# Norm stage of a decoder layer: transfers in another order, last row sums taken singly, first row in column thirds

## The reference, cut to what matters

```python
mod = jax.nn.silu(c) @ p['w_ada'] + p['b_ada']
sh_m, sc_m, g_m, sh_f, sc_f, g_f = [m[:, None, :] for m in jnp.split(mod, 6, axis=-1)]
xn = rmsnorm(x, p['rms_mix_g']) * (1.0 + sc_m) + sh_m
mix, k_rows, v_rows, s_new = token_mixer(xn, pos, p, attend, recur)
```

## Time and profile before

| | us |
|---|---|
| median of 3 runs | 2231.82 (2231.39 to 2233.82) |
| profiled execution, own time | 2233.89 |
| profiled execution, span from first to last instruction | 2232.1 |
| TensorE busy in the span | 2204.0 |
| mean granted TensorE clock | 0.999 of full speed |

### The profile page before, as it was taken

How to read it: one execution, slowest core, us unless ns; L and a number is a source line. 1 busy time by engine, 2 the same in 40 slices (tenths; PEclk the granted TensorE clock), 3 DMA queues, 4 the chain that set the end, 5 groups by cost and what they waited for, 6 DMA issues and landing times. The chain is left out here.

```text
span 2232.1 us, 48427 instructions
## 1 busy us (share of the span) xinstructions
PE 2204.0 (99%) x19103; PEld 2118.4 (95%) x19103; DVE 1517.7 (68%) x2529; ACT 1204.8 (54%) x2499; POOL 988.5 (44%) x1186
## 2 busy tenths in 40 slices
PE   7999999999999999999999999999999999999999
PEld 6899999999999999999898999999999999999999
DVE  5767677776767676775767425318988888876534
ACT  6667676767767676766443421125566666644110
POOL 1147272745555472727322124441256565635431
PEclk9999999999999999999999999999999999999999
DMA  8222222122222222222789523112354555485212
GB/s 311 67 65 81 67 88 67 59 87 76 80 71 85 74 72 68 88 67 97 299 307 363 212 51 124 38 57 94 122 185 174 188 185 191 172 313 193 86 48 96
DMA packets 103515, 288.37 MB, mean 129 GB/s; under 512 B 18426, under 2 KB 26490, under 8 KB 103290
## 3 DMA queue, kind: packets, MB, share of 16 engines
q1 hardware_dynamic: 102138, 281.09, 35.6%
q10 hardware_dynamic: 1152, 4.19, 0.5%
HBM read 213.18 MB, written 63.77 MB: 124 GB/s over the span
## 5 line engine op out<-in xcount | busy, mean ns | idle before, releaser
L173 PE MATMUL ps<-xn_hi,h_w_hi 128*128 128x344 f32 x1680 | 550.1, 327 | 2.3 <-PEq L206 0.9
L173 PE MATMUL ps<-xn_lo,h_w_hi 128*128 128x344 f32 x1680 | 536.6, 319 | 0.0
L173 PE MATMUL ps<-xn_hi,h_w_lo 128*128 128x344 f32 x1680 | 536.5, 319 | 0.0
L173 PEld LDWEIGHTS ps<-xn_hi,h_w_hi 128*128 128x128 f32 x1680 | 317.1, 189 | 20.7 <-issue 12.8
L173 PEld LDWEIGHTS ps<-xn_lo,h_w_hi 128*128 128x128 f32 x1680 | 315.8, 188 | 0.6
L173 PEld LDWEIGHTS ps<-xn_hi,h_w_lo 128*128 128x128 f32 x1680 | 315.8, 188 | 0.0
L1314 POOL TENSOR_TENSOR h_w_lo<-h_w_raw,h_w_hi 128x1024 fp32r<-128x1024 f32 x58 | 139.9, 2413 | 356.7 <-DVE h_a_E L1528 192.2
L3279 DVE SCALAR_TENSOR_TENSOR x<-ps,keep_mod,x 128x344 f32<-128x344 f32 x168 | 94.1, 570 | 162.6 <-PE ps L3116 99.7
L3116 PE MATMUL ps<-f_act_lo,f_d_hi 128*128 128x344 f32 x528 | 169.4, 321 | 0.0
L3116 PE MATMUL ps<-f_act_hi,f_d_lo 128*128 128x344 f32 x528 | 168.8, 320 | 0.0
L3116 PE MATMUL ps<-f_act_hi,f_d_hi 128*128 128x344 f32 x528 | 168.4, 319 | 0.2 <-DVE x L3279 0.2
(11 more groups left out here) (494 smaller groups left out, 6706.9 us busy)
## 6 DMA issues: line engine op xcount, KB each, us to landing
h_w_raw<-in_w_in SPq DMA_DIRECT2D x72, 512.0 KB, 3.5
y_rows<-f_y SPq DMA_DIRECT2D x44, 516.0 KB, 2.6
f_y_pair<-y_rows SPq DMA_DIRECT2D x22, 1032.0 KB, 5.3
h_d_ada_w<-in_w_ada SPq DMA_DIRECT2D x32, 512.0 KB, 3.8
g_vp<-in_cache_v SPq DMA_DIRECT2D x32, 512.0 KB, 6.0
f_a<-in_w_ffn SPq DMA_DIRECT2D x57, 256.0 KB, 2.6
g_kp<-in_cache_k SPq DMA_DIRECT2D x28, 512.0 KB, 7.8
h_w_raw<-in_w_mix SPq DMA_DIRECT2D x24, 512.0 KB, 3.5
```

Of the source, the lines that this page charges most:

```text
L173: ins = eng.matmul(out, w[:, k * P:(k + 1) * P], x[:, k, columns], start=(k == 0 and n == 0), stop=(k == n_k - 1 and n == 2))
```

## The change

- Transfers: x's rows 2 to 7 in one go; then the vectors, ada(0), the first two weights and ada(1) to ada(7), and all else behind them.
- Sums: pairs 0 to 2 as before; rows 6 and 7 are summed by TensorE each for itself.
- ScalarE rounds weight 0 (`split(0)`) between read_ada(0) and add_bias(0), no longer between the squares; VectorE rounds weight 1; weight 2 is rounded behind row 3. The two exponentials of the small vectors move behind row 4, VectorE's part of them (`exponents`, `bounds`) to rows 3 and 6.
- Row 0 is multiplied, rounded, reduced to its remainder and multiplied by the weights by column thirds, and stands in TensorE's list ahead of ada(2) and ada(3). VectorE copies ada(1) out of PSUM.
- ScalarE now does add_bias(k + 1) and read_ada(k + 2) behind row k.

```diff
-            load_x(2)
-            load_x(3)
-            load_w(0)
-            for k in range(4, KT):
+            for k in range(2, KT):
                 load_x(k)
             sp.dma_start(c["vec"][:, :], a["vec"]).then_inc(vec_in.sem, 16)
+            load_ada(0)
+            load_w(0)
             load_w(1)
-            load_ada(0)
-            for k in range(1, 5):
+            for k in range(1, KT):
                 load_ada(k)
...
-            split(0)
             for k in range(4, KT):
                 square(k)
-            act.wait_ge(lam_s.sem, 1)
-            act.activation(c["lam"][:, 0:2], c["lam"][:, 4:6], ACT.Exp).then_inc(lam_e.sem, 1)
-            act.wait_ge(lb_s.sem, 1)
-            act.activation(lw[:, 3:5, :], lw[:, 1:3, :], ACT.Exp).then_inc(lb_e.sem, 1)
-            split(1)
...
             read_ada(0)
-            read_ada(1)
+            split(0)
             add_bias(0)
-            read_ada(2)
-            add_bias(1)
             for k in range(KT):
...
+                if k == 0:
+                    for j in range(NP):
+                        act.activation(hi[:, 0, cols(j)], x[:, 0, cols(j)], ACT.Copy).then_inc(high.sem, 1)
+                else:
+                    act.activation(hi[:, k, :], x[:, k, :], ACT.Copy).then_inc(high.sem, 1)
                 if k == 1:
+                    read_ada(2)
+                if k + 1 < KT:
+                    add_bias(k + 1)
+                if 0 < k and k + 2 < KT:
+                    read_ada(k + 2)
+                if k == 3:
                     split(2)
...
+            def row_sums(k):
+                pe.wait_ge(squared.sem, k + 1)
+                for j in range(NP):
+                    ins = pe.matmul(SP_[:, j, 0:TH], mean[:, :], sq[k % 4][:, cols(j)], start=False, stop=(k == KT - 1))
+                    if k == KT - 1:
                         ins.then_inc(summed.sem, 1)
...
+            def first_pieces():
+
+                for t in range(2):
+                    pe.wait_ge(w_hi.sem, t + 1)
+                    pe.wait_ge(w_lo.sem, t + 1)
+                    for j in range(NP):
+                        pe.wait_ge(high.sem, j + 1)
+                        pe.wait_ge(low.sem, j + 1)
+                        row_products(0, t, j)
+                    if t == 0:
+                        pick(1)
...
-            for p in range(KT // 2):
+            for p in range(KT // 2 - 1):
                 sums(p)
+            row_sums(KT - 2)
+            row_sums(KT - 1)
             pe.wait_ge(csil.sem, 1)
             ada(0)
-            keep_clock(2)
-            ada(1)
+            keep_clock(3)
             pe.wait_ge(pick_ready.sem, 1)
             pick(0)
+            keep_clock(8)
+            ada(1)
             keep_clock(2)
+            pe.wait_ge(lnd.sem, NP)
+            first_pieces()
             ada(2)
-            keep_clock(1)
-            pick(1)
-            keep_clock(3)
-            pe.wait_ge(lnd.sem, NP)
-            for k in range(KT):
+            pick(2)
+            ada(3)
+            for k in range(1, KT):
                 if k + 3 < KT:
                     ada(k + 3)
...
             def rows(k):
 
-                ch(dve.tensor_tensor(x[:, k, :], x[:, k, :], rs[:, :], ALU.mult))
+                if k == 0:
+                    for j in range(NP):
+                        dve.wait_ge(rstd.sem, j + 1)
+                        ch(dve.tensor_tensor(x[:, 0, cols(j)], x[:, 0, cols(j)], rs[:, cols(j)], ALU.mult))
+                else:
+                    ch(dve.tensor_tensor(x[:, k, :], x[:, k, :], rs[:, :], ALU.mult))
+                if k == 1:
+                    dve.wait_ge(ada_done.sem, 2)
+                    copy(dve, av[1][:, :], X[:, 1, 0:2 * P]).then_inc(ada_read.sem, 1)
+                    rest(0)
...
             rows(0)
+            dve.wait_ge(w_in[1].sem, 16)
+            dve.wait_ge(w_hi.sem, 1)
+            copy(dve, early["hi"][1][:, :], early["raw"][1][:, :]).then_inc(w_hi.sem, 1)
             for k in range(1, KT):
                 rows(k)
-                rest(k - 1)
+                if k > 1:
+                    rest(k - 1)
+                if k == 3:
+                    exponents()
+                if k == 6:
+                    bounds()
```

More of the change, by code:

```diff
@@ L265, in _ @@
                 sp.dma_start(c[n][:, :], a[n]).then_inc(kept.sem, 16)
-            load_ada(5)
             for n in ("blk", "cos"):
@@ L337, in _ @@
                 act.wait_ge(scaled.sem, k + 1)
-                act.activation(hi[:, k, :], x[:, k, :], ACT.Copy).then_inc(high.sem, 1)
-                if k == 1:
-                    split(2)
[L341 to L344, removed]
+                if k == 0:
[3 more added lines that the diff above has]
+                    act.activation(hi[:, k, :], x[:, k, :], ACT.Copy).then_inc(high.sem, 1)
+                if k == 1:
+                    read_ada(2)
[4 more added lines that the diff above has]
+                if k == 3:
+                    split(2)
+                if k == 4:
+                    act.wait_ge(lam_s.sem, 1)
+                    act.activation(c["lam"][:, 0:2], c["lam"][:, 4:6], ACT.Exp).then_inc(lam_e.sem, 1)
+                    act.wait_ge(lb_s.sem, 1)
+                    act.activation(lw[:, 3:5, :], lw[:, 1:3, :], ACT.Exp).then_inc(lb_e.sem, 1)
         @block.tensor
@@ L350, in sums @@
                 for j in range(NP):
-                    ins = pe.matmul(SP_[:, j, 0:TH], mean[:, :], sq[2 * p % 4][:, cols(j)], start=(p == 0), stop=(p == KT // 2 - 1))
-                    if p == KT // 2 - 1:
+                    ins = pe.matmul(SP_[:, j, 0:TH], mean[:, :], sq[2 * p % 4][:, cols(j)], start=(p == 0), stop=False)
+                ins.then_inc(ms_used.sem, 1)
+            def row_sums(k):
[3 more added lines that the diff above has]
+                    if k == KT - 1:
                         ins.then_inc(summed.sem, 1)
-                if p < KT // 2 - 1:
-                    ins.then_inc(ms_used.sem, 1)
             def ada(k):
@@ L379, in keep_clock, with row_products @@
                     pe.matmul(G[:, 0, 0:P], mean[:, :], mean[:, :], start=True, stop=True)
-            def pieces(k):
[L383 to L391, removed]
+            def row_products(k, t, j):
+                n, w = EARLY_PIECES.index((t, j)), slice(k * P, (k + 1) * P)
+                for q, (wp, xp) in enumerate(((early["hi"], hi), (early["hi"], lo), (early["lo"], hi))):
+                    pe.matmul(first[n], wp[t][:, w], xp[:, k, cols(j)], start=(k == 0 and q == 0), stop=(k == KT - 1 and q == 2))
@@ new lines, in first_pieces @@
+            def first_pieces():
[8 more added lines that the diff above has]
+                        pick(1)
+            def pieces(k):
+                pe.wait_ge(high.sem, k + NP)
+                pe.wait_ge(low.sem, k + NP)
+                for t, j in EARLY_PIECES:
+                    row_products(k, t, j)
@@ L403, in _ @@
+            first_pieces()
             ada(2)
-            keep_clock(1)
-            pick(1)
-            keep_clock(3)
-            pe.wait_ge(lnd.sem, NP)
-            for k in range(KT):
+            pick(2)
+            ada(3)
+            for k in range(1, KT):
                 if k + 3 < KT:
                     ada(k + 3)
-                if k == 0:
-                    keep_clock(1)
                 if k + 2 < KT:
                     pick(k + 2)
-                if k == 0:
-                    keep_clock(6)
@@ L448, in _ @@
             dve.wait_ge(vec_in.sem, 16)
[L449 to L473, removed]
-            def rows(k):
-                ch(dve.tensor_tensor(x[:, k, :], x[:, k, :], rs[:, :], ALU.mult))
+            def exponents():
+                lv = vec[:, VEC["lam"][0]:VEC["lam"][0] + 4 * DH].rearrange("p (c s n) -> p c s n", c=2, s=2)
+                ch(dve.tensor_tensor(tmp[:, :, :], lv[:, :, 0, :], lv[:, :, 1, :], ALU.mult))
+                ch.sync()
+                dve.tensor_reduce(c["lam"][:, 4:6], tmp[:, :, :], AX.X, ALU.add).then_inc(lam_s.sem, 1)
+                lb0 = VEC["lb"][0]
+                l0, l1 = vec[:, lb0:lb0 + H], vec[:, lb0 + H:lb0 + 2 * H]
+                ch(dve.tensor_tensor(lw[:, 0, :], l0, l1, ALU.max))
+                ch.sync()
+                ch(dve.tensor_tensor(lw[:, 1, :], l0, lw[:, 0, :], ALU.subtract))
+                dve.tensor_tensor(lw[:, 2, :], l1, lw[:, 0, :], ALU.subtract).then_inc(lb_s.sem, 1)
@@ new lines, in bounds @@
+            def bounds():
+                dve.wait_ge(lam_e.sem, 1)
+                ch(dve.tensor_tensor(c["lam"][:, 2:3], c["lam"][:, 0:1], c["lam"][:, 1:2], ALU.subtract))
+                ch.sync()
+                ch(dve.tensor_scalar(c["lam"][:, 2:3], c["lam"][:, 2:3], LAM_INIT, None, ALU.add))
+                ch.sync()
+                ch(dve.tensor_scalar(c["lam"][:, 3:4], c["lam"][:, 2:3], -1.0, None, ALU.mult))
+                dve.wait_ge(lb_e.sem, 1)
```

(19 more changed lines are left out.)

2 lines of the change are left out of this document (removed).

## The result

The changed kernel takes 2237.86 us (median of 14 runs, 2236.11 to 2239.38), the kernel before 2233.33 (14 runs, 2230.96 to 2234.32): ratio 1.0023, interval 1.0015 to 1.0030, slower by 3.4 to 6.7 us (5.1 by the ratio, 4.5 between the two medians). The profiled execution has a span of 2236.3, against 2232.1.

The account below looks back on a forecast made before the run. The prediction took the norm stage to be bound by a latency chain to the first product at 31.91, then a packed TensorE list. +5.2 us at stage end, +7.0 with the clock, gave 2238.8 us, eight-in-ten range 2232.9 to 2241.3.

Parts of the forecast that it names:

- Break-even: TensorE after the first product: 2.9 us more work there, so the first product must come 2.9 us earlier.
- Step 1: Sums and root: single sums add a TensorE group; first logarithm at 21.7 instead of 21.10, +0.6 us.
- Step 2: Transfers in their new order: nothing gained or lost, zero.
- Steps 3 and 4: Row 0: add_bias(0) ends at 26.3; VectorE/GpSimd lock holds of 1.9 and 2.2 us; first product at 33.5, 1.6 later.
- Step 5: First product to pieces(1): ScalarE/VectorE chain makes TensorE wait 1.5 us before pick(2); pieces(1) at 42.2 instead of 36.38, +5.8.
- step 7: TensorE's clock falls in the wait before the first product; first products and pick(1) at half pace, +1.8 us (0 to 5).
- Step 6: Tail from pieces(1): same 26.9 us list, old waits gone -1.0, 0.4 back; stage end 68.4, +5.2 us.
- The sum: Norm stage's end: +5.2 us without the low clock, +7.0 with it.
- (B): Rival: lock does not hold the chain; first product 29.6, end about +1.2, 2233.0 us, no change; chance 0.17.
- (C): Rival: clock stays at 1.2 GHz through the stretch with waits, +5.2 + 5, about 2242 us; chance 0.08.
- (D): Rival: faster; lock and pick(2) both hidden, TensorE packed from 29.6, stage end 62.9, 2229.8 us; chance 0.03.

Follow-up runs that it names:

- run 2: Changed kernel with weights 0 and 1 loaded ahead of ada(0) and both rounded on ScalarE between squares and root: 2232.05 us, ratio 1.0003 to the kernel before.
- run 8: The kernel before, unchanged, profiled a second time: one run, third group of sums at 16.56 us, stage end at 62.59 us.
- run 7: Changed kernel with only the sums undone, four pairs of squares again: 2236.23 us, ratio 1.0019 to the kernel before.
- run 3: Changed kernel with only weight 0 loaded and rounded where the kernel before had it, weight 1 still on VectorE: 2235.86 us, ratio 1.0017 to the kernel before.
- run 1: Changed kernel with sixteen turns of keep_clock instead of two ahead of the first products: 2234.97 us, ratio 1.0014 to the kernel before.
- run 4: As run 2, with ada(1), ada(2), pick(1) ahead of the first products and ada(1)'s copy, add_bias(1), read_ada(2) earlier: 2229.30 us, 0.9989 to the kernel before.
- run 5: Changed kernel with only ada(2) moved ahead of the first products: 2237.39 us, ratio 1.0024 to the kernel before.
- run 6: As run 4, with the last two rows summed as a pair again and ada(2) behind pick(1): 2228.86 us, ratio 0.9987 to the kernel before.

## Why the prediction was right

- **Break-even.** The 2.9 us were there, and more: from the first product to the stage's end the kernel before takes 31.36, run 2 34.81. The 3.45 between them are the 2.9 and the wait of 1.32 before pick(2), less the 0.8 by which the later waits are shorter (0.84 and 0.19 before, 0.22 after). Counted from the third group of sums, run 2 brings the first product 2.55 earlier and ends 0.9 later.
- **Step 1** had the sign and not the size: the first logarithm came at 21.27, not 21.7. Counted from the start of the third group it came after 4.35, against 4.04 before (3.85 in run 8): +0.3 to +0.5 for +0.6. The pace of the groups was right (1.84 for 1.85), and the first third's sum was ready sooner than I allowed. Run 7 shows what the change gave away in it, 1.0 us, because nothing else holds the root up once split(1) is gone from ScalarE.
- **Step 2** held: after the first four rows of x no wait of TensorE, VectorE, ScalarE or GpSimd in the stage after is for a transfer.
- **Steps 3 and 4** held. add_bias(0) ended at 25.79 (26.3), the first hold is 1.9 us (1.9), the rounding of weight 1 took 0.69 (0.7), lo(1) went ahead of the thirds and ran to 32.30 (33.0), and the first product stands at 32.82 (33.5): 0.5 early by steps 1 and 3, 0.2 in the hand-overs. Runs 2 and 3 show that the holds do it. The rule of the Trainium skill (SBUF — State Buffer, "Who interferes with whom") agrees in both halves: the operations that share the pair ended behind GpSimd's (line 509 by 0.04 us, the first remainder third by 0.37), and the copy with its one PSUM input was not held (0.42 here and 0.42 alone in run 2). That lo(1) needed the copy to get its turn, as the prediction has it, is not borne out: the third remainder got its turn with no copy between. It had waited since 49.82 and ran when row 3's remainder on VectorE ended at 50.38, and row 5's multiply, which starts at 50.29 right behind, was held. In both places GpSimd's operation had been waiting first; the prediction's other reason, the subtraction at 34.65, was the sound one.
- **Step 5** had the mechanism, but the wait before pick(2) was 0.50 and not 1.5: the low clock of step 7 stretched the products that stand ahead of it. With the clock up (run 1) it is 1.32. Runs 4 and 5 show the chain over ScalarE behind it.
- **Step 6** held: 25.9 us from pieces(1) to the end (26.2), with 0.22 of waiting left (0.4) and the third hold hidden.
- **Step 7** held: low from 31.2 to 38, worth 1.6 by run 1 (1.8).
- **The sum** was 7.0 at the stage end, that is 70.3; the trace gives 69.20, 5.9 more than before and 6.1 counted from the third group of sums. Of the 1.1 that the forecast was too high, 0.7 are there at the first product and 0.3 in step 6. The time moved by 4.5 to 5.1 (3.4 to 6.7), which agrees with 6.1 and does not reach 7.0. The forecast time of 2238.8 is nearer to the measured 2237.86 than that, and this is luck: the forecast was added to a median of three runs, 2231.82, and over fourteen runs the kernel before reads 2233.33. A term that the prediction did not have is the low clock near 82 us in the profile that it started from. It belongs to the execution (run 8), so that a difference between two single profiles is uncertain by about 1.5 us.
- **Rivals.** (B) falls with the first product at 32.82, (C) with the clock back at 38, (D) with both; runs 4 and 6 show that the first half of (D), holds and pick(2) gone, is to be had by another order, at about 0.1%.

## What to carry to other kernels

Before moving an operation to VectorE or GpSimd, lay both engines' lists beside one another in time: two subtractions that had lain where VectorE idled cost about 5 us with their consequences once they lay on its critical operations (run 2), though neither engine was busy more than 68% of the span. A step moved ahead of others helps only if what it displaces does not come back behind it: fill the waits with the displaced work (run 4), or nothing is gained (run 2). A wait taken out by more work on the engine that ends last (single sums instead of an addition) is no wait taken out (run 7). And before two profiles are compared, look for a mark that stands behind the same work in both: here the front of the executions differed by up to 1 us.

## What the runs showed of the hardware

- A GpSimd subtraction that was waiting for VectorE got its turn as soon as the operation ahead of it ended, even with VectorE's next one right behind. This shows at 30.09, where a copy out of PSUM lay between (VectorE's next operation then waited 1.8 us), and at 50.38, where nothing did (a multiply took 3.41 instead of 1.23).
- The granted clock fell to 0.50 during or behind waits of TensorE of 4.03 us (changed kernel), 4.01 (run 7), 3.01 and 1.71 (run 5) and 2.08 (run 3). It did not behind 1.32 (runs 1 and 2), 1.21 (run 7), nor behind the 1.72 ahead of the third group of sums before. The length of the wait alone does not decide, as 1.71 and 1.72 show; near 80 to 90 us the clock fell in one profile of the kernel before and not in the other, behind the same wait.
